# The expert stage rewritten, with the third group of w2 loaded ahead of the next expert's first pair

## The reference

```python
def ec_moe(h, router_w, w1, w3, w2):
    cap = EC_CAPACITY_FACTOR * n // N_EXPERTS            # 2 * 256 // 16 = 32
    affinity = jax.nn.softmax((h @ router_w).astype(jnp.float32), axis=-1)
    gate, idx = lax.top_k(jnp.swapaxes(affinity, 1, 2), cap)
    xg = jax.vmap(lambda hb, ib: hb[ib])(h, idx)
    hid = jax.nn.silu(einsum('becd,edf->becf', xg, w1)) * einsum('becd,edf->becf', xg, w3)
    out = einsum('becf,efd->becd', hid, w2) * gate[..., None]
    return jax.vmap(lambda ob, ib: zeros((n, d)).at[ib.reshape(-1)].add(ob.reshape(-1, d)))(out, idx)

def channel_sublayer(x, mod, ng, router_w, w1, w3, w2):
    h = modulate(rmsnorm(x, ng[2]), mod[3], mod[4])
    return x + mod[5] * rmsnorm(ec_moe(h, router_w, w1, w3, w2), ng[3])
```

## Time and profile before

| | us |
|---|---|
| median of 3 runs | 3579.72 |
| lowest and highest | 3577.03, 3583.22 |
| the profiled execution's own time | 3568.94 |
| its span, from first to last instruction | 3567.2 |
| PE, DVE, ACT, POOL busy | 2644.9, 888.8, 523.7, 299.6 |

### The profile page before, as it was taken

The page is one execution under the profiler, slowest core; times in us unless marked ns, Lnnn a source line. Parts: engine busy times, 40 slices in busy tenths (PEclk is TensorE's granted clock), DMA queues, the critical chain, the costliest instruction groups (busy, mean ns, idle before and its releaser), DMA issues. The chain is left out here.

```text
span 3567.2 us, 55702 instructions
## 1 busy us (share of the span) xinstructions
PE 2644.9 (74%) x23142; PEld 1365.3 (38%) x23142; DVE 888.8 (25%) x1895; ACT 523.7 (15%) x1076; POOL 299.6 (8%) x345
## 2 busy tenths in 40 slices
PE   4399966274958787777849577777778587777777
PEld 0144424142433222222324376777777322222222
DVE  1104015454021111111150055444445201000001
ACT  0100021321030000000020033332333100000000
POOL 0000000250010000000010222222222000000000
PEclk9899988696979999999979898888889799999999
DMA  9621100000218999999612300000000389999996
GB/s 383 260 73 71 71 0 1 0 1 24 83 66 329 414 413 414 414 403 414 255 40 71 116 12 12 12 12 12 12 12 3 119 342 413 413 413 411 404 409 255
DMA packets 180052, 676.24 MB, mean 190 GB/s; under 512 B 28568, under 2 KB 46784, under 8 KB 175344
## 3 DMA queue, kind: packets, MB, share of 16 engines
q1 hardware_dynamic: 178704, 672.45, 47.5%
q10 hardware_dynamic: 1120, 0.48, 0.0%
HBM read 666.35 MB, written 6.49 MB: 189 GB/s over the span
## 5 line engine op out<-in xcount | busy, mean ns | idle before, releaser
L1361 PE MATMUL bank<-moe_w,moe_xT 128*64 128x512 f32 (+3 forms) x3072 | 664.4, 570 | 223.8 <-DMA moe_w<-in_exp_w 221.6
L1361 PEld LDWEIGHTS bank<-moe_w,moe_xT 128*64 128x64 f32 (+1 forms) x3072 | 181.6, 124 | 711.0 <-DMA moe_w<-in_exp_w 378.2
L1381 PE MATMUL bank<-moe_w,moe_hidT 128*64 128x512 f32 (+1 forms) x1408 | 331.3, 628 | 15.1 <-ACT moe_hidT L1415 11.8
L1440 DVE TENSOR_TENSOR moe_silu<-bank,moe_silu 64x512 f32<-64x512 f32 (+3 forms) x96 | 56.6, 639 | 840.3 <-ACT moe_silu L1409 840.3
L1409 ACT ACTIVATE moe_silu<-bank 64x512 f32<-64x512 f32 (+3 forms) x96 | 46.2, 545 | 1218.0 <-PE bank L1361 1218.0
L1381 PEld LDWEIGHTS bank<-moe_w,moe_hidT 128*64 128x64 f32 (+1 forms) x1408 | 97.9, 128 | 223.9 <-issue 216.6
L391 PE MATMUL bank<-w_slab,mixT 128*128 128x512 f32 x384 | 166.2, 593 | 1.8 <-PE bank L391 1.5
L2048 PE MATMUL bank<-x_inv_and_t,p_prod 64*64 64x64 f32 x2560 | 154.1, 219 | 7.5 <-issue 6.6
L1454 DVE COPY moe_rows<-bank 32x512 f32 (+1 forms) x96 | 65.9, 686 | 356.0 <-PE bank L1381 355.1
L1810 DVE TENSOR_TENSOR x_inv_and_t<-bank,x_inv_and_t 128x512 f32<-128x512 f32 (+1 forms) x160 | 102.1, 638 | 194.3 <-PE bank L2048 193.6
L388 PE MATMUL bank<-mixT,w_slab 128*128 128x512 f32 x320 | 140.7, 601 | 12.2 <-DMA w_slab<-in_ab_w_in 11.1
(11 more groups left out here) (449 smaller groups left out, 3162.9 us busy)
## 6 DMA issues: line engine op xcount, KB each, us to landing
moe_w<-in_exp_w SPq DMA_DIRECT2D x512, 704.0 KB, 10.9
moe_w<-in_exp_w SPq DMA_DIRECT2D x352, 512.0 KB, 14.9
ada_slab<-in_ada_w SPq DMA_DIRECT2D x32, 1536.0 KB, 12.8
w_slab<-in_ab_w_in SPq DMA_DIRECT2D x11, 2048.0 KB, 7.4
wo_slab<-in_ab_w_out SPq DMA_DIRECT2D x16, 512.0 KB, 3.6
rw_slab<-in_rw_wk SPq DMA_DIRECT2D x4, 1024.0 KB, 6.6
rw_slab<-in_rw_wv SPq DMA_DIRECT2D x4, 1024.0 KB, 4.9
rw_slab<-in_rw_wr SPq DMA_DIRECT2D x4, 1024.0 KB, 4.8
```

What stands on the lines that cost most here:

```text
L1361: mm = pe.matmul(g.ps[k][64 * m:64 * m + M, 0:hi - lo], xg[:, j, c, :], wa[:, c % RA, m, lo:hi], start=(c == 0), stop=(c == DC - 1))
L1381: mm = pe.matmul(g.ps[5 + m][64 * m:64 * m + M, :], hidt[:, c, :], wb[:, c % RB, 512 * m:512 * m + 512], start=(c == 0), stop=(c == FC - 1))
```

## The change

The stage is written anew; the mixers and the first loads' place in the program are as before. What it does:

- **Loads.** w1/w3 come as four *pairs* of chunks instead of eight chunks: a partition takes rows 8p + 2c and 8p + 2c + 1 as one run of 11,264 bytes (5,632 before), so a pair is two DMAs of 1,408 KB. w2 comes as three *groups* of 4, 4 and 3 chunks, one DMA each of 2,048, 2,048 and 1,536 KB with runs of 16,384 and 12,288 bytes (4,096 before). The buffers are three slots for pairs (pairs 0, 1, 2, 3 in slots 0, 1, 2, 0) and two for groups (groups 0, 1, 2 in slots 0, 1, 0). To fit the rows' new order, picks and transposes read their stationary operand with a stride of 8 and 11 elements.
- **Order.** Per expert SP issues pairs 1, 2, 3, groups 0, 1, 2, then pair 0 of the next expert. Group 2 waits for PE to have used group 0 of the same expert, pair 3 for pair 0.
- **First loads.** Three pairs and two groups of expert 0 are issued at the start of the stage, and behind them the modulation's columns (32 bytes per partition).
- **Norm and router** are one block. Norm runs tile by tile; half of the modulation is on DVE; the router's weights are the stationary operand, padded to 32 columns, and the logits are transposed afterwards. Rows are picked from the normed tokens without modulation, and the modulation is applied to the picked rows on DVE, so the transposes back are gone. `sel` alone is made here; its weighted form and the transposes for `selt` are moved into the first experts.
- **Picks** run four at a time after every fourth expert, into banks 7, 0, 1 and 2: one at once, three after the product of silu is made.
- **Tail.** The sums over the first three blocks of experts are made during the last four experts (`early`) and kept in SBUF; after the last expert only one matmul per half tile is left. Squares, root, gain and addition go tile by tile over ACT, POOL and DVE.
- The loops over blocks of four experts are unrolled.

```diff
-    RA, RB = 4, FC
+    PAIR_SLOT, PAIR_VISIT, VISITS = (0, 1, 2, 0), (1, 1, 1, 2), (2, 1, 1)
+    GROUP_SLOT, GROUP_VISIT, GVISITS, GROUP = (0, 1, 0), (1, 1, 2), (2, 1), ((0, 4), (4, 8), (8, FC))
+        def pair_in(sp, e, c):
+            for k, w in enumerate((w1, w3)):
+                sp.dma_start(wa[:, PAIR_SLOT[c], k, :, :].rearrange("p r f -> p (r f)"),
+                             w[e].rearrange("(p c) f -> p (c f)", c=DC)[:, 2 * c * FF:2 * (c + 1) * FF]).then_inc(s_wa[PAIR_SLOT[c]], 16)
+
+        def group_in(sp, e, c):
+            lo, hi = GROUP[c]
+            sp.dma_start(wb[:, GROUP_SLOT[c], 0:hi - lo, :].rearrange("p r n -> p (r n)"),
+                         w2[e].rearrange("(p c) n -> p (c n)", c=FC)[:, lo * D:hi * D]).then_inc(s_wb[GROUP_SLOT[c]], 16)
...
+                for c in range(3):
+                    pair_in(sp, 0, c)
+                for c in range(2):
+                    group_in(sp, 0, c)
+                for s in segs:
+                    for k in range(2):
+                        sp.dma_start(modc[:, s, k, :], g.modp[...]).then_inc(s_modc, 16)
...
+                dve.wait_ge(s_modc, 32 * ns)
+                for n, s in enumerate(segs):
+                    dve.wait_ge(s_bc, n + 1)
...
+                def pair(e, c):
+                    if c == 3:
+                        sp.wait_ge(s_ua, 4 * e + 1)
+                    else:
+                        sp.wait_ge(s_ua, 4 * (e - 1) + (c + 1 if c else 4))
+                    pair_in(sp, e, c)
+
+                def group(e, c):
+                    if c == 2:
+                        sp.wait_ge(s_ub, 3 * e + 1)
+                    elif e:
+                        sp.wait_ge(s_ub, 3 * (e - 1) + 3 - c)
+                    group_in(sp, e, c)
+
+                for e in range(NE):
+                    if e:
+                        pair(e, 1)
+                        pair(e, 2)
+                    pair(e, 3)
+                    if e:
+                        group(e, 0)
+                        group(e, 1)
+                    group(e, 2)
+                    if e + 1 < NE:
+                        pair(e + 1, 0)
...
-                    pick(i + 1, j, 8 * (i + 1) + 2 * j)
+                    if j == 3 and i < NB - 1:
...
+                        pick(i + 1, 0)
+                        pe.wait_ge(s_hid, e + 1)
+                        for q in range(1, 4):
+                            pick(i + 1, q)
+                    if i == NB - 1:
+                        early(j, 0)
                     pe.wait_ge(s_hid, e + 1)
-                        mm = pe.transpose(..., hid[:, c * P:(c + 1) * P], g.ident[0:M, 0:M])
+                        mm = pe.transpose(..., hid[:, c::FC], g.ident[0:M, 0:M])
+                    for gr, (lo, hi) in enumerate(GROUP):
+                        sl = GROUP_SLOT[gr]
+                        pe.wait_ge(s_wb[sl], 16 * (GVISITS[sl] * e + GROUP_VISIT[gr]))
...
+                        mm.then_inc(s_ub, 1)
...
-                        for b in range(NB):
-                            mm = pe.matmul(g.ps[2 * (t - t0) + h][:, :], selt[:, s, b, ...], oe[:, s, b, 512 * h:512 * h + 512], ...)
+                        mm = pe.matmul(g.ps[2 * n + h][:, :], selt[:, t // 2, NB - 1, ...], oe[:, t // 2, NB - 1, 512 * h:512 * h + 512], start=True, stop=True)
```

More of the change, by code:

```diff
@@ L1167, in stage_moe @@
+        s_wa, s_wb = [g.sem(f"moe_w13_{i}") for i in range(3)], [g.sem(f"moe_w2_{i}") for i in range(2)]
+        (s_rw, s_rwz, s_modc, s_sq, s_root, s_xn, s_tp, s_eva, s_evd, s_lg, s_lgc, s_lgt, s_max, s_e, s_aff, s_at, s_bd, s_bc, s_own) = (g.sem("route_" + n) for n in (
+            "weights", "weights_zeroed", "mod_cols", "squares", "root", "xn", "transposed", "out_scalar", "out_vector", "logits", "logits_kept", "logits_turned", "max", "exp", "affinity", "rows", "diag", "spread", "own"))
         with nc.Block() as block:
@@ new lines, in _ @@
+                sp.wait_ge(s_ua, 4 * (NE - 1) + 2)
+                for st in range(2):
+                    if st == 1 and t0:
+                        continue
+                    sp.dma_start(gain[:, st, :], g.modp[layer, st:st + 1, 5 * D:6 * D].broadcast_to([P, D])).then_inc(s_tgain, 16)
+                if out is not None:
+                    for n in range(nt):
+                        sp.wait_ge(s_add, n + 1)
+                        sp.dma_start(out[0, n * P:(n + 1) * P, :], g.x[:, t0 + n, :]).then_inc(s_store, 16)
+                    sp.wait_ge(s_store, 16 * nt)
@@ L1401, in _, with keep @@
             @block.scalar
             def _(act):
-                def expert(i, j, first):
-                    e = i * 4 + j
-                    act.wait_ge(s_ua, (e + 1) * DC)
-                    if not first:
+                def keep(j, n):
+                    t, h = EARLY[j][n]
+                    act.wait_ge(s_cm, first_of[j] + n + 1)
+                    act.activation(acc[:, t, 512 * h:512 * h + 512], g.ps[7][:, :], ACT.Copy).then_inc(s_cmo, 1)
+                for e in range(NE):
+                    i, j = e // 4, e % 4
+                    act.wait_ge(s_ua, 4 * (e + 1))
+                    if e:
@@ new lines, in _ @@
+                    if i == NB - 1 and len(EARLY[j]) > 1:
+                        keep(j, 1)
+                for n, t in enumerate(range(t0, NT)):
+                    act.wait_ge(s_acc, 2 * n + 2)
+                    act.activation(tsq[:, t, :], acc[:, t, :], ACT.Square, accum_out=tssq[:, 0, t:t + 1]).then_inc(s_tsq, 1)
+                    act.wait_ge(s_tsq, n + 1)
+                    act.activation(tssq[:, 1, t:t + 1], tssq[:, 0, t:t + 1], ACT.Sqrt, bias=g.eps[:, 0:1], scale=1.0 / D).then_inc(s_troot, 1)
```

507 lines of the change are left out of this document (257 added, 250 removed).

## The result

The changed kernel takes 3799.59 us, the median of four runs (3794.36 to 3806.51), against 3579.76 for the kernel before on the same chip: ratio 1.0615, 95% interval 1.0594 to 1.0635. It is slower, by the wait that the prediction named, but by 220 us where 110 were forecast. The median lies 0.4 us inside the upper end of the range (3635 to 3800), and two of the four runs (3801.99, 3806.51) lie outside it. The profiled execution has a span of 3795.2, 228.0 more than before.

The account below looks back on a forecast made before the run. Group 2's wait for group 0 was to empty the load queue in each expert. Layer 0 +42 and layer 1 +65 made +107 on 3568.94: 3676, or 3687 on the median's scale, forecast 3690 us, range 3635 to 3800.

Parts of the forecast that it names:

- the wait that the prediction named: SP's load of group 2 waits for PE to use group 0; the queue empties, +81 us in each layer.
- The cycle without picks: Expert stages, one opening of group 2's wait to the next: 47.8 us against 42.4 before, +5.4 per expert.
- the opening: Moment when PE has used group 0 and SP may issue group 2; pair 3 lands about 33.3 us later.
- X: Time from pair 3 landing to w2's group 0 used: 14.5 us, bounds 12.7 to 16.2.
- PE at 1.2 GHz through pair 3: Rival, expert stages: waits let PE's clock fall for pair 3 too, cycle 55.4, +228, 3915 us; chance 0.08.
- The strided operands: Rival, picks and transposes: strided weight loads take twice their time, about 3755 us; chance 0.15.
- three of 16 instructions at 2.05 = 6.1: Picks after the product in every fourth expert of layer 0 lengthen X; +4.3 each net of a warmer PE.
- The 4.2 from w1/w3 to w2: Part of X from the end of w1/w3 to the first w2 instruction: silu, product, transposes and copy, 4.2 us.
- the lower rate: Bound on the expert loads: 412 GB/s instead of 425, 1.1 us per cycle more, +33.
- a colder w2: Bound on X: all 16 w2 instructions at half speed, +3.5, X 16.2; with 30 cycles +51.
- Router: Stage start to first expert: modulation columns decide at +34.2 in layer 0; -21.5 us there, -2.6 in layer 1.
- Tail: After the last w2: sums and norm tile by tile with engines overlapping, -25.5 us in layer 0, -10.8 in layer 1.

Follow-up runs that it names:

- E2: Changed kernel with a third slot for w2's group 2 in layer 1 alone, strict order kept: 3653.01 us, ratio 1.0211.
- E3: Changed kernel with picks and transposes reading stationary operands without stride, rows matched wrongly so output is not the reference's: 3725.06 us, ratio 1.0419.
- E5: Kernel before with its loops over blocks of experts unrolled in Python, nothing else: 3573.67 us, ratio 0.9982.
- E8: Kernel before with 40 PE instructions that do nothing at the end of layer 0's expert stage: 3580.64 us, ratio 1.0003.
- E6: Changed kernel with eight filler matmuls ahead of the wait for the product in experts 4, 5, 6, 8, 9, 10 of each layer: 3762.90 us, ratio 1.0510.
- E8 to E11: PE no-ops after layer 0's stage: 40 in E8; then 192 in the changed kernel (3804.07 us), 192 in E7 (3518.27), 96 in the changed kernel (3797.52).
- E4: Changed kernel with rows in the old order (shorter runs, no strides) and modulation columns taken from those already in SBUF: 3737.42 us, ratio 1.0460.
- E1: Changed kernel with the next expert's pair 0 issued ahead of group 2: 3610.40 us, ratio 1.0093.
- E7: Changed kernel, layer 0 with E4's rows and E1's order, layer 1 with E2's slot and modulation columns loaded before the weights: 3524.44 us, ratio 0.984.

## Why the forecast was right in kind and half in size

**The bound and the wait: right.** The queue runs empty behind groups 0 and 1 in every cycle, the DMA share is 0.78 and 0.83 (0.85 forecast), and E2 takes just this wait away and gets 40.7 us per expert. That is also the 17.30 MB/425 that the prediction used for the long runs.

**The cycle without picks: 47.8 forecast, 49.5 and 48.5 measured.** Two terms held nearly as they were: from the opening to group 2's matmul (6.05 to 6.58, 6.1 forecast), and from the first w2 instruction to the opening (3.5 + 1.8 forecast; in layer 0 5.0 to 5.4 in seven turns, 6.0 to 6.6 in four and 3.7 in five). Experts 12 to 14, with the early sums in the wait, have an X of 13.4 (12.7 forecast), the others of layer 0 without picks 14.5 to 16.5. Two terms were short. From the opening to pair 3 it took 33.2 to 34.9, mean 34.1 over the 30 cycles, where 33.3 was forecast. And PE at 1.2 GHz through pair 3, which stood as a rival for every turn, came in some: 6.64 instead of 4.94, so +1.7, in experts 6 and 9 of layer 0 and (6.61) 3 and 7 of layer 1, 7.77 in the last expert of layer 0 and 6.31 in expert 14 of layer 1. In six other turns of layer 0 it was pair 1 or 2 that took 6.64, and pair 3 behind it 4.94, on time. As a rule for every turn the rival would have given cycles of 55.4, which no distance without picks reached; the argument against it (PE's clock in the rows of before with the same share of work) was right for most turns only. The Trainium skill, "TensorE: Matmul & The Clock Gate", HAM oscillation, describes a kernel that begins every tile cold after its DMA wait. The trace agrees in part: pair 0 took over 6.2 in all of layer 1's turns behind the first and 7.4 to 7.7 in six of layer 0's fifteen, but 4.94 or 4.95 in the other nine, and pair 3 mostly was not cold.

**The strided operands: the term that failed.** The prediction put them at nothing in its sum and kept them as a rival with 0.15, at 3755. They are real: 0.242 us per pick against 0.128, 1.55 against 0.87 for eleven transposes. E3, which differs by them alone, is 75 us faster, of which 66.3 lie in the stages; the rival's sum was +67. The step that failed is thus "three of 16 instructions at 2.05 = 6.1", made to +4.3 for an expert with picks: three of 16 at 3.9 are 11.6, and the distances rose by 11.6 over their neighbours in layer 0 (+4.3 forecast) and by 5.5 in layer 1 (+1.3). The 4.2 from w1/w3 to w2 kept the old transposes too, whose time rose by 0.7. In E3, without strides, layer 0's distances with picks are 52.4, 52.1 being the forecast. The Trainium skill, "SBUF — State Buffer", Door 1: The DMA port swizzle, says that an access which goes to a new 16-byte line each time pays. The trace agrees, and here the instructions take nearly twice their time.

**What is left of the gap.** The profiled executions differ by 228.1 us where the terms gave 106.6. Of the 121.5 missing, 66.3 are the strides. Another 27.4 are distances: E3's add up to 1467.9 where the prediction's terms give 1440.5 (the cold pairs and the later landing). The last 27.8 are layer 1's mixer. What else the starts and ends missed by cancels out.

**That the time fell into the range is luck.** Its upper end was made of this wait with the strides, the lower rate and a colder w2. The lower rate didn't come (E2 shows 422 GB/s for these runs), and in its place came the cold pairs and some 20 us of a mixer that no term spoke of. The 1.1 per cycle that the prediction took for 412 GB/s should also have been 1.0 (30.9 us of transfers, 3% longer).

**Router: right in kind, 6 us short in layer 0.** The columns decided, as forecast:

```profile
1049.95 2.73 DVE L1328 TENSOR_SCALAR moe_pick<-bank,token_number 128x512 f32<-128x512 f32 x4 [8.20 <-DMA moe_mod_cols<-mod_rows]
...
1053.22 15.51 PE L1387 MATMUL bank<-moe_pick,moe_xn 128*128 128x128 f32 x64 [9.33 <-PEq L1191]
```

They were there 34.0 after the start (34.2 forecast). The picks behind them took 15.5 instead of 9.9, the strides once more.

**Tail: right, 5 us short in layer 0.** POOL's multiplication of a tile was taken at 2.5:

```profile
1895.28 2.36 POOL L1554 TENSOR_TENSOR moe_xn<-moe_xn,moe_w 128x1024 f32<-128x1024 f32 x1 [878.53 <-ACT moe_w L1490]
...
1897.85 3.39 POOL L1554 TENSOR_TENSOR moe_xn<-moe_xn,moe_w 128x1024 f32<-128x1024 f32 x1 [0.21 <-ACT moe_w L1490]
...
1901.48 3.36 POOL L1554 TENSOR_TENSOR moe_xn<-moe_xn,moe_w 128x1024 f32<-128x1024 f32 x1 [0.24 <-ACT moe_w L1490]
```

The first, with DVE nearly idle beside it, takes 2.36, the later ones 3.34 to 3.39, and they are the chain. Beside each of the later ones runs DVE's addition L1541, 1.28 long; that it is the cause was not tested. The covers and leftovers that were put at nothing (unrolling, `selt`, the moved picks) cost nothing that E5 or the table shows.

**Layer 1's mixer: not foreseen, and its cause is open.** Its code is the same. The window over it, after:

```profile
1912.10:2952.00 1039.90, 770.26 (x15376) 621.77 (x15376) 411.58 (x747) 268.22 (x535) 192.98 (x252) 0.88 0.10 32
```

and before:

```profile
1803.90:2816.06 1012.16, 766.18 (x15376) 619.08 (x15376) 411.55 (x747) 267.75 (x534) 193.44 (x250) 0.88 0.10 33
```

Every engine does the same work at the same clock (PE 4 us more of it), and all idle longer. Part of it is the profiled execution of before, which lies 10.8 under the median: E5 and E8, with the old stage, have 1020.9 and 1019.4. All runs with the new stage have 1034 to 1046, but E6 1022. So about 20 of the 220 us belong to this, as far as one profiled execution per kernel can tell. Over half of the difference stands in one of PE's waits, for which the profile shows no releaser (total us, times, longest), before and after:

```profile
PE bank L1977 <- issue: 38.2, 13, 5.9
PE bank L2059 <- issue: 54.1, 19, 6.1
```

Another 9.4 us are of the same kind in front of L2114 (11.4, and 2.0 at L2032 before). The lag grows step by step: 258 us into the mixer both kernels are level within 0.3 us, at 816 us the changed one is 27.5 behind, and it stays so. Unrolled loops (E5) and the places of the loop that E8 to E11 tried don't explain it. What in the new stage does, and what E6 changes in it, was not found; other addresses of the buffers were not tried.

## What to carry to other kernels

When loads are issued in order, look for a wait on the *same* iteration's compute: everything issued behind it inherits that wait, and its price per turn is the time from the last landed load to the release, less what the queue still holds, plus the restart of the empty queue. Longer runs helped little here (E4, under 1 us per expert); one more place does (8.9 us of 49.6), or issuing an independent load ahead (E1, about 6).

A layout that makes DMA runs longer may make another engine's reads strided. Price both: here the runs won 0.5 to 0.9 us per expert, and the reads cost 0.6 in an expert without picks and 8.6 (61.0 against 52.4) in one of layer 0 with them, where the queue waited for PE. With the slot of E2 the same slow reads were free in layer 1.

## What the runs showed of the hardware

- A 128x128 fp32 stationary operand read at a stride of 8 elements: 0.242 us per instruction at a granted clock of 1.00, against 0.128 in a row (rows 6; 0.141 in E3 from a standing start); 11 transposes at a stride of 11 elements: 1.55 to 1.60 in layer 0, against 0.86 to 0.87 before.
- Loads in long runs (11 to 16 KB) sustained 422 to 424 GB/s where the queue stayed full (E2, E7), against 411 to 412 with 5.6 and 4 KB. In E1, with long runs and the engines busy for 0.97 to 0.98 of four stretches inside the stages, they moved 404 to 409.
- The granted clock fell around waits as short as 2.0 us (pair 2 of layer 0's expert 12, 6.64 instead of 4.94) and not around others of 3.5 (pair 0 of expert 4, 4.94). 2 us of filler matmuls gave w2 its 7.09 back from 8.78 in eight of twelve turns.
- POOL's 128x1024 multiplication: 2.34 to 2.36 with DVE nearly idle, 3.34 to 3.39 with DVE's L1541 beside it.
- An untouched stretch took 1012 to 1046 us in thirteen programs, with equal counts of instructions and nearly equal busy times where they were compared (before and after).
